# Two transformer blocks on one core: V with tokens on partitions, one table set for Ln and Exp, other evictions and sums

## The reference, cut to what matters

```python
def rmsnorm(x, g):
    y = xf * lax.rsqrt(jnp.mean(xf * xf, axis=-1, keepdims=True) + EPS)
...
        h = rmsnorm(x, pre_mix_norm[l])
        z = h @ w_in[l]
...
        kv = (rmsnorm(kv_lat, kv_norm[l]) @ w_ukv[l]).reshape(B, S, N_HEADS, QK_NOPE + V_HEAD)
        k_nope, v = kv[..., :QK_NOPE], kv[..., QK_NOPE:]
...
        x = x + rmsnorm(mix, post_mix_norm[l])
        hf = rmsnorm(x, pre_ffn_norm[l])
        ff = (jax.nn.silu(hf @ w_gate[l]) * (hf @ w_up[l])) @ w_down[l]
        x = x + rmsnorm(ff, post_ffn_norm[l])
```

## Time and profile before

| what | us |
|---|---|
| median of 3 runs | 2812.18 (2811.93 to 2817.59) |
| profiled execution, its time | 2814.44 |
| its span | 2812.7 |
| TensorE busy (share) | 2582.6 (92%) |
| VectorE busy | 1723.7 (61%) |
| ScalarE busy | 1321.3 (47%) |

### The profile page before, as it was taken

How to read it: one execution, slowest core, us unless ns; L and a number is a source line. 1 busy time by engine, 2 the same in 40 slices (tenths; PEclk the granted TensorE clock), 3 DMA queues, 4 the chain that set the end, 5 groups by cost and what they waited for, 6 DMA issues and landing times.

```text
span 2812.7 us, 38385 instructions
## 1 busy us (share of the span) xinstructions
PE 2582.6 (92%) x14428; PEld 2223.0 (79%) x14428; DVE 1723.7 (61%) x2457; ACT 1321.3 (47%) x1836; POOL 15.6 (1%) x34
## 2 busy tenths in 40 slices
PE   6979687999999999979989768898899999999997
PEld 5868476888888888868878548787688888888886
DVE  5889466665665644475775435456677676775454
ACT  4456455544444443454444432346564454544342
POOL 0000000000000000000010000000000000000000
PEclk9989689999999999999989858999999999999999
DMA  6543044555655555535565200154255556555453
GB/s 203 173 132 120 0 135 134 180 185 188 193 182 192 189 185 183 190 127 188 183 200 185 97 0 1 46 180 165 92 165 193 186 187 193 182 192 190 169 195 119
DMA packets 235581, 435.91 MB, mean 155 GB/s; under 512 B 14040, under 2 KB 32488, under 8 KB 235360
## 3 DMA queue, kind: packets, MB, share of 16 engines
q1 hardware_dynamic: 232368, 424.02, 46.3%
q0 software_dynamic: 1968, 6.44, 0.6%
q10 hardware_dynamic: 1152, 4.19, 0.4%
HBM read 432.51 MB, written 3.68 MB: 155 GB/s over the span
## 4 chain that ended last, share of the span: by engine, by line
PE 83%; DVE 11%; ACT 3%; issue 1%; DMA 1%; SPq 0%; DVEq 0%; ACTq 0%
PE ps L639 49%; PE ps L644 24%; DVE w_lo L403 3%; PE ps L1199 1%; DVE ar L942 1%; PE ps L966 1%; DVE x L748 1%; PE ps L1547 1%; PE ps L1179 1%; PE ps L1026 1%; PE ps L802 1%; PE ps L1544 1%; DVE ar L481 1%; PE ps L1538 1%; PE ps L1054 1%
## 5 line engine op out<-in xcount | busy, mean ns | idle before, releaser
L639 PE MATMUL ps<-x,w_hi 128*128 128x512 f32 x5064 | 1614.7, 400 | 89.9 <-DVE x L748 60.9
L403 DVE TENSOR_TENSOR w_lo<-w_raw,w_hi 128x1024 fp32r<-128x1024 f32 (+3 forms) x820 | 986.4, 1209 | 805.0 <-ACT w_hi L397 804.3
L397 ACT ACTIVATE w_hi<-w_raw 128x1024 fp32r<-128x1024 f32 (+3 forms) x820 | 853.4, 1046 | 1036.5 <-PE ps L644 1006.6
L644 PEld LDWEIGHTS ps<-x,w_lo 128*128 128x128 f32 x5064 | 963.0, 190 | 228.2
L644 PE MATMUL ps<-x,w_lo 128*128 128x256 f32 x5064 | 1006.0, 280 | 0.0
L639 PEld LDWEIGHTS ps<-x,w_hi 128*128 128x128 f32 x5064 | 783.2, 191 | 99.0 <-issue 73.2
L639 PE MATMUL ps<-h,w_hi 128*128 128x512 f32 x1408 | 442.5, 396 | 4.7 <-DVE w_lo L403 4.7
L644 PEld LDWEIGHTS ps<-h,w_lo 128*128 128x128 f32 x1408 | 264.5, 188 | 62.5
L644 PE MATMUL ps<-h,w_lo 128*128 128x256 f32 x1408 | 276.6, 278 | 0.0
L639 PEld LDWEIGHTS ps<-h,w_hi 128*128 128x128 f32 x1408 | 214.3, 189 | 5.3 <-issue 4.4
L417 ACT ACTIVATE half<-ps 128x256 f32<-128x256 f32 x380 | 142.4, 380 | 79.2 <-PE ps L644 76.1
(11 more groups left out here) (255 smaller groups left out, 1359.4 us busy)
## 6 DMA issues: line engine op xcount, KB each, us to landing
w_raw<-in_w_gate SPq DMA_DIRECT2D x88, 1024.0 KB, 5.2
w_raw<-in_w_up SPq DMA_DIRECT2D x88, 1024.0 KB, 5.1
w_raw<-in_w_down SPq DMA_DIRECT2D x88, 1024.0 KB, 5.1
w_raw<-in_w_in SPq DMA_DIRECT2D x80, 1024.0 KB, 5.1
w_raw<-in_w_out SPq DMA_DIRECT2D x32, 1024.0 KB, 5.1
w_raw<-in_w_xkv SPq DMA_DIRECT2D x8, 1024.0 KB, 5.0
w_raw<-in_w_uq SPq DMA_DIRECT2D x18, 256.0 KB, 3.7
w_raw<-in_w_ukv SPq DMA_DIRECT2D x16, 256.0 KB, 3.9
```

The source lines that it names most:

```text
L397: nc.scalar.activation(w_hi[:, u % HIS, 0:ks.stop - ks.start, cs], w_raw[:, slot(g, j), ks, cs], ACT.Copy)\
L403: nc.vector.tensor_tensor(w_lo[:, slot(g, j), ks, cs], w_raw[:, slot(g, j), ks, cs], w_hi[:, u % HIS, 0:ks.stop - ks.start, cs].bitcast(F3 ...
L639: nc.tensor.matmul(bank, w_hi[:, u % HIS, k - ks.start, c0:c0 + P], both.rearrange("p a n -> p (a n)"), start=(n == 0 and k == 0), stop=False)
L644: ins = nc.tensor.matmul(bank[:, T:2 * T], w_lo[:, slot(g, j), k, c0:c0 + P], hi, start=False, stop=(final and k == ks.stop - 1))
```

## The change

- V's products (the last two groups of `ukv` and of `qkv_b`, the second of `xkv`) are made in a form "swap": x is the stationary operand (128 tokens), the weights move, 512 columns at a time, and V lands with tokens on partitions. The turning of V and its copies go. The norm's factor is now one number a partition; GpSimd takes the row through DRAM to get it as a column (`column_pool`). VectorE evicts such a group with two multiplications of 512 elements, ScalarE does nothing.
- Other evictions take two banks in one instruction, on ScalarE and VectorE.
- The groups go on alternating between the two halves of the banks from one product to the next where these are named; before, every product began in its own fixed half.
- Ln and Exp use one table set that holds both, loaded ahead of Ln. The Newton step takes three instructions, not four.
- For `w_out`, `down` and `down_2` the sum over partitions of the parts that are ready is made two units before the product's end, the last part after it. Their second turn and the turns of `qkv_b` are written out.
- `add_norm` takes chunks 0 and 1 singly, 2 and 3 together, the rest in fours, with the low parts right behind the additions.
- `rel_pe` and the first group of `qkv_b` wait no longer for the last group of `z_ba`.

```diff
-            Gemm("ukv", 1, [group(w_heads(A["w_ukv"], 256, h0, 4, off, 128), 1, banks=b, out=(ar, at + h0, 0), parts=4)
-                            for b, h0, off, at in ((4, 0, 0, K1), (0, 4, 0, K1), (4, 0, 128, V1), (0, 4, 128, V1))],
-                 lambda k: x2c(6 + k), rs_kv),
-            Gemm("w_out", 2, [group(w_loop(A["w_out"], 0 + b * P, 2 * W), 4, banks=b, out=(ar, M1 + b, 8), kind="sum")
+            Gemm("ukv", 1, [group(w_heads(A["w_ukv"], 256, h0, 4, 0, 128), 1, out=(ar, K1 + h0, 0), parts=4) for h0 in (4, 0)] +
+                           [group(w_heads(A["w_ukv"], 256, h0, 4, 128, 128), 1, out=(ar, VN1 + h0 // 2, H // 2), kind="v", parts=4)
+                            for h0 in (4, 0)],
+                 lambda k: x2c(6 + k), rs_kv, column=0),
...
-            Gemm("qkv_b", 3, [group(w_loop(A["w_in_2"], 4112 + b * P, 2 * W), 4, banks=b, out=(ar, ZB + b, 8))
-                        for b in (0, 4)], x2c, rs_x),
-            Gemm("w_out_2", 2, [group(turned(w_loop(A["w_out_2"], b * P, 2 * W)), 4, banks=b, out=(xt, 0 + b, 8), kind="add")
+            Gemm("qkv_b", 1, [group(w_cols(A["w_in_2"], 4112 + k * W, W), 4, out=(ar, ZB + 4 * k, 0)) for k in range(4)] +
+                             [group(w_cols(A["w_in_2"], 4112 + (4 + k) * W, W), 4, out=(ar, VN2 + 2 * k, H // 2), kind="v") for k in range(2)],
+                 x2c, rs_x, column=1),
...
+            if g.name not in ("latents", "ukv", "down", "z_ba", "qkv_b", "down_2"):
+                side = 0
             for k, gr in enumerate(g.groups):
-                gr["t"], gr["e"], gr["n"] = at, bank, k
+                gr["form"] = "swap" if gr["kind"] == "v" else g.form
+                gr["t"], gr["e"], gr["n"] = at, 2 * k, k
+                gr["banks"] = (4 if g.form == "wide" else 2) * side
+                side = 1 - side
                 at += gr["tiles"]
...
+                for b in range(2):
+                    c, n, h, banks = pair(gr, b)
+                    group_ready(act, g, i, gr, b)
+                    nc.scalar.activation(half[:, c:c + n, h], banks[:, :, h], ACT.Copy).then_inc(half_out, 1)
...
+            if kind == "v":
+                where, base_c, step = gr["out"]
+                dve.wait_ge(col_in, 16 * (g.column + 1))
+                for t in range(TT):
+                    group_ready(dve, g, i, gr, t)
+                    c = base_c + t * step
+                    nc.vector.tensor_scalar(where[:, c:c + 2, :].rearrange("p c t -> p (c t)"), ps[:, gr["banks"] + t, :],
+                                            rs_col[:, g.column, t:t + 1], None, ALU.mult).then_inc(evicted, 1)
...
-                xc = lambda m: chunk(xt, base_c + m, step, i)
-                for m in range(M):
-                    dve.wait_ge(half_out, e + m + 1)
-                    nc.vector.tensor_tensor(xc(m), xc(m), ps[:, gr["banks"] + m, T:2 * T], ALU.add)\
-                        .then_inc(add_half, 1)
-                a0 = g.a0 + gr["e"] + i * g.banks
-                for m in range(M):
-                    dve.wait_ge(add_half, a0 + m + 1)
-                    nc.vector.tensor_tensor(xc(m), xc(m), half[:, m, :], ALU.add).then_inc(bank_free, 1)
+                for b in range(2):
+                    c, n, _, banks = pair(gr, b)
+                    x = chunk(xt, base_c + c, step, i, n)
+                    dve.wait_ge(half_out, h0 + b + 1)
+                    nc.vector.tensor_tensor(x, x, banks[:, :, T:2 * T], ALU.add).then_inc(add_half, 1)
+                a0 = g.a0 + gr["e"] + i * g.ops
+                for b in range(2):
+                    c, n, _, _ = pair(gr, b)
+                    x = chunk(xt, base_c + c, step, i, n)
+                    dve.wait_ge(add_half, a0 + b + 1)
+                    nc.vector.tensor_tensor(x, x, half[:, c:c + n, :], ALU.add).then_inc(evicted, 1)
...
+                    if gr["form"] == "swap":
+                        for t in range(TT):
+                            bank = ps[:, gr["banks"] + t, :]
+                            tok = slice(t * P, (t + 1) * P)
+                            for k in range(ks.start, ks.stop):
+                                nc.tensor.matmul(bank, x(k)[:, 0, tok], w_h(k, slice(0, W)),
+                                                 start=(n == 0 and k == 0), stop=False)
+                                nc.tensor.matmul(bank, x(k)[:, 1, tok], w_h(k, slice(0, W)), start=False, stop=False)
+                                nc.tensor.matmul(bank, x(k)[:, 0, tok], w_l(k, slice(0, W)), start=False,
+                                                 stop=(final and k == ks.stop - 1)).then_inc(products, 1)
...
+            if g.name in STREAM_STAT:
+                assert g.turns == 2
+                name, last = STREAM_STAT[g.name], g.groups[-1]
+                at = 2 * last["t"] + 6
+                body(1, 0, at)
+                pe.wait_ge(evicted, evicted_by(g, 1, g.groups[-2]))
+                sum_pe(pe, name, 0, STATS[name][2] - 1)
+                body(1, at)
+                sum_pe(pe, name, STATS[name][2] - 1)
+            elif g.turns > 1:
...
+            act.preload_act_table_set(LN_EXP)
...
-            for _ in range(2):
-                dve_chain.link(dve, nc.vector.tensor_tensor(st_v[:], st_v[:], st_y[:], ALU.mult))
-            dve_chain.link(dve, nc.vector.tensor_scalar(st_v[:], st_v[:], -0.5, 1.5, ALU.mult, ALU.add))
-            nc.vector.tensor_tensor(dst, st_v[:], st_y[:], ALU.mult).then_inc(st_done, 1)
+            newton(dve, st_v[:], st_y[:], dst).then_inc(st_done, 1)
...
+        def newton(dve, v, y, dst):
+            dve_chain.link(dve, nc.vector.scalar_tensor_tensor(v, v, -0.5, y, ALU.mult, ALU.mult))
+            dve_chain.link(dve, nc.vector.tensor_tensor(v, v, y, ALU.mult))
+            return nc.vector.scalar_tensor_tensor(dst, v, 1.5, y, ALU.add, ALU.mult)
...
-            pairs0 = a.first // 2
-            for hp in range(a.heads // 2):
-                n = pairs0 + hp
-                if n >= 2:
-                    pe.wait_ge(v_kept, n - 1)
-                for k in range(TT):
-                    for hh in range(2):
-                        last = nc.tensor.transpose(ps[:, 4 + n % 2, (2 * k + hh) * P:(2 * k + hh + 1) * P],
-                                                   ar[:, a.v + 2 * hp + hh, k * P:(k + 1) * P], ident[:])
-                last.then_inc(v_turned, 1)
...
-            pairs0 = a.first // 2
-            for hp in range(a.heads // 2):
-                n = pairs0 + hp
-                act.wait_ge(v_turned, n + 1)
-                nc.scalar.activation(vn(a)[:, :, 2 * hp:2 * hp + 2, :],
-                                     ps[:, 4 + n % 2, :].rearrange("p (k h d) -> p k h d", k=TT, h=2),
-                                     ACT.Copy).then_inc(v_kept, 1)
...
+        def column_pool(pool, n, row, name):
+            pool.wait_ge(st_done, STATS[name][0] + 1)
+            pool.dma_start(rs_d[n:n + 1, :], row[0:1, :]).then_inc(col_out, 16)
+            pool.wait_ge(col_out, 16 * (n + 1))
+            pool.dma_start(rs_col[:, n, :], rs_d[n:n + 1, :].rearrange("a (t p) -> p (a t)", p=P),
+                           allow_slow_non_contiguous=True).then_inc(col_in, 16)
...
+            act.preload_act_table_set("natural_log")
...
-                for k in range(DC // 4 + 1):
-                    if k < DC // 4:
-                        apply(dve, src, 4, 4 * k)
-                        for c in range(4 * k, 4 * k + 4):
-                            nc.vector.scalar_tensor_tensor(xt[:, c, :], src(c), col(gain, c), xt[:, c, :],
-                                                           ALU.mult, ALU.add).then_inc(x_added, 1)
-                    if k:
-                        prep_dve(dve, prep, xs, gain_of(pgain), prep, 4 * (k - 1), 4)
-            dve.sem_inc(bank_free, AHEAD_B)
+                def add(c0, n):
+                    apply(dve, src, n, c0)
+                    for c in range(c0, c0 + n):
+                        nc.vector.scalar_tensor_tensor(xt[:, c, :], src(c), col(gain, c), xt[:, c, :],
+                                                       ALU.mult, ALU.add).then_inc(x_added, 1)
+                def low(c0, n):
+                    prep_dve(dve, prep, xs, gain_of(pgain), prep, c0, n)
+                n0 = apply.n
+                add(0, 1)
+                add(1, 1)
+                low(0, 1)
+                add(2, 2)
+                low(1, 1)
+                low(2, 2)
+                for c in range(4, DC, 4):
+                    add(c, 4)
+                    low(c, 4)
+                assert apply.n == n0 + ADDS
...
-            sum_pe(pe, "mix")
...
-            pe.wait_ge(bank_free, AHEAD_B + G["z_ba"].e0 + 8)
+            pe.wait_ge(evicted, G["qkv_b"].e0 - 2)
```

267 lines of the change are left out of this document (158 added, 109 removed).

## The result

| | before | changed |
|---|---|---|
| median of 4 runs, us | 2812.80 (2811.93 to 2817.59) | 2795.32 (2793.94 to 2796.05) |
| ratio, 95% interval | | 0.9934 (0.9917 to 0.9951) |
| profiled execution, its span | 2814.44, 2812.7 | 2796.02, 2794.2 |
| TensorE busy, rest of the span | 2582.6, 230.1 | 2587.3, 206.9 |

The account below looks back on a forecast made before the run. TensorE, 92% busy, was taken to bound the kernel. The terms -16.3 - 10.5 - 3.7 - 3.1 + 0.75 + 7.3 sum to -25.6 us, giving 2786.5 us against the median of 2812.18; range 2774 to 2800.

Parts of the forecast that it names:

- (a): Norm chains: the table load between Ln and Exp goes, the Newton step shortens; 1.6 us a chain, -16.3 us.
- (b): Before the scores of latent, block and cross-attention: the turning of V goes, -10.5 us.
- (c): Cheaper evictions of V: -2.5 us in `ukv` before `rope_pe`, -1.2 in `xkv` before `xq`; -3.7 us in all.
- (d): From `z_ba` to `qkv_b`: TensorE needs only the first of three low halves and starts sooner, -3.1 us.
- (f): `add_norm` at mix and ff: single first chunks start the product earlier, but the next sum waits and the clock falls, +7.3 us.
- (e): Evictions in pairs of banks come later, early sum passes shorten products' ends; both nearly cancel, +0.75 us.
- R1: The forecast itself, all terms as summed: 2774 to 2797 us, chance 0.55.
- R2: Single first chunks in `add_norm` cost nothing, the clock stays up: 2776 to 2783 us, say 2779; chance 0.22.
- R3: Around delta rule, convolution's norms and attentions, other work eats part of the gain, 9 to 11 us: 2797 us, chance 0.2.
- R4: V's matmuls in the swap form show their weight loads, 64 us over 336 matmuls: 2850 us, chance 0.03.

Follow-up runs that it names:

- V the old way: The changed kernel with V made as before (channels on partitions, turned by TensorE, kept by ScalarE, no factor through DRAM): 2807.74 us, ratio to before 0.9982.

## Why the prediction was right, and where it was short

The direction, the range and most of the waits held; 17.5 us came of 25.6. By the medians the change splits in three: table set and Newton 15.0 (forecast (a) 16.3), V 12.4 (forecast (b) and (c) 14.2), and what remains, (d) to (f), cost 9.9, where +4.95 was forecast. This split takes it that the parts add up, which no run shows, and each part carries some 4 us of interval and of the clock's scatter. So the traces, place by place, say more.

- **(a)** right in the waits. Those at kv, 4.56 to 2.95, and at the head norms l2, 5.59 to 3.99, and moba, 4.33 to 2.74, shrank by 1.6 each. The rule of the Trainium skill that was weighed ("ScalarE: Activation LUTs", What ACT_TABLE_LOAD costs) would have made it 2.66 a chain; 17.9 us over 14 norms say 1.28.
- **(b)** right at its places: 3.1, 4.8 and 2.1 us against 3.1, 5.1 and 2.3. At cross-attention more is lost behind the scores than is won in front of them.
- **(c)** too large in `ukv`: the wait before `rope_pe` went from 3.59 to 2.45, 1.1 instead of 2.5. I had let the savings of both V groups reach the end. But `rope_pe` never waited for the last group's multiplication by the row (L491). VectorE's rows for that last eviction, before and changed:

```profile
254.77 1.40 DVE L481 TENSOR_TENSOR ar<-half,ps 128x256 f32<-128x256 f32 x4
256.21 1.22 DVE L491 TENSOR_TENSOR ar<-ar 128x1024 f32<-128x1024 f32 x1
250.37 1.40 DVE L502 TENSOR_SCALAR ar<-ps,rs_col 128x512 f32<-128x512 f32 x2
```

`rope_pe` started at 256.32, when the additions were done; they took 1.40 us, and the two multiplications now take the same. What is won comes from the group before it, whose eviction fell from 2.6 to 1.3 us, so that the splits behind it end sooner. In front of `xq` the wait fell from 4.29 to 3.40, 0.9 us of the 1.2.
- **(d)** right at its place, 4.86 to 1.82, 3.0 us. But the waits for low halves in the last units of `z_ba` grew by 1.0 us, which the forecast did not have, so 2.0 arrive. The wait of 1.23 or 1.24 stands in every run built on the changed kernel, and 0.75 in the two built on that before; the smaller part beside it varies from run to run. No run tells what makes it.
- **(e)** right in size at the ends (3.37 to 3.69, two passes of 1.22), the whole not separable.
- **(f)** right, and the step that decided R1 against R2: forecast a wait of 4.9 and a sum of 3.24, measured 5.55 and 3.75; undoing it gave 8.1 us against 7.3.
- **The step that failed** is one that (a) to (e) share: each took the clock outside the norms as unchanged. The sum was built from waits, and waits did nearly what it said (23.2 us less); the clock took most of the rest. From cross-attention's scores to the sum in `ffn_2` it cost 4.8 us, and that V's turning had held it up there is shown by the run "V the old way". At the start of `down` it cost 1.1, behind a wait of 1.85 us where before it had held behind 2.04. In block attention and the delta rule, where the chains at l2 and moba gave 1.6 each, the time from the scores to `w_out_2` shrank by 0.4 only. Behind `rope_pe` the clock gave 1.7 back and at the start of `xq`, behind the shorter wait, 1.1. How much of the loss in block attention belongs to the change stays open: the same 1028 matmuls took from 170.5 to 180.5 us in the kernels of this study.
- **R3** had nearly the size (9 to 11 us) with, in the main, the wrong reason: it looked for other work in the way, and of that only the 1.0 us in `z_ba` is found.
- **R4** is out: 0.23 us a matmul. The rule that was weighed, of the Trainium skill on row groups ("TensorE: Matmul & The Clock Gate", Part 3: Packing small matmuls, row/col tiling), isn't what this form shows. The same section also names a load into the background weight buffer as one that is pulled ahead; that case would fit the rows.

## What to carry to other kernels

Where one engine must end a whole pass before a later sum, an earlier start in front of it only moves the wait; shorten what the pass does before the sum, and keep a cover for each cross-engine wait inside it. On a TensorE-bound kernel count two things apart, the time in which it stands and the time in which it works, since a change can win in the first and lose in the second. Work that nobody reads, put into a wait before dense work, can pay: in the 2.71 us before cross-attention it brought 6.1 us. It is not a rule: before block attention the same brought nothing, and at q and kv what it won was lost in the next stage. And taking out work that looked useless for the time, like the turning of V, can cost clock behind it.

## What the hardware showed beyond what I expected

The same program ran at different mean clocks from execution to execution: of the kernel before, one of 2806.1 us at 0.955 and one of 2818.7 at 0.947. Much of such a difference can sit in one stage: the 1028 matmuls from block attention's scores to `w_out_2` were busy for 177.6 us in the kernel before and for 170.5 with the table set alone. The granted clock after a wait of one length isn't fixed either: `rope_pe` took 1.97 or 3.55 us behind a wait of 2.45, and the same eight passes after 3.37 to 3.38 us took 1.97 in the earlier trace rows and 3.60 in the run with the table set alone (timeline of TensorE, "ff"):

```profile
1210.83 3.60 PE L802 MATMUL ps<-ssq,ones 128*128 128x256 f32 x8 [3.38 <-DVE ssq L546]
```

So a forecast of such a kernel has a few us of clock in it that no count of waits gives. And V's form with x as the stationary operand is slightly faster by the column than the other: 0.2275 us for 512 columns (1.365 for six matmuls) against 0.2325, about 1.7 us over the 336.
